# Starting the next token group's input projection beside the current group's top-k and routing

## The chip, the cores and the metric

One core of a Trainium2 chip runs the whole program. The metric is the device time of one execution in microseconds (us). TensorE (PE) does the matrix products, VectorE (DVE) elementwise work, reductions and top-8 searches, ScalarE (ACT) activations and copies, GpSimd (POOL) issues the gathers of expert rows, and SyncE (SP) issues nearly all other transfers. The matrices are float32.

## The reference, cut to what matters

One decoder layer is applied to 512 prompt tokens and 64 sample tokens. Each token's row of 2048 numbers passes through an input projection, two mixers (latent attention and gated linear attention), an output projection, the PEER expert layer and a gated embedding.

```
xn = rmsnorm(x, norm_mix);  z = xn @ w_in                      # 2048 x 3920, split for the two mixers
mix = concat(mla(z), gla(z)) @ w_out;  h = x + mix
xf = rmsnorm(h, norm_ffn)                                       # PEER:
q = (xf @ peer_w_q)                                             # 8 heads x 2 sides x 128
s1, s2 = q[:, :, 0] @ keys1.T, q[:, :, 1] @ keys2.T             # 128 scores for each head and side
v1, i1 = top_k(s1, 16);  v2, i2 = top_k(s2, 16)
top_s, sel = top_k(v1 + v2 (16 x 16 sums), 16)
e = i1[sel // 16] * 128 + i2[sel % 16];  gate = softmax(top_s)
h = h + sum over head, k of gate * gelu(xf . peer_u[e]) * peer_v[e]   # 128 gathered row pairs for each token
y = h + sigmoid(rmsnorm(h) @ w_ple_gate) * (p @ w_ple_proj)
```

## The kernel before, in words

**Tiles and groups.** The 576 tokens are five tiles: tiles 0 to 3 hold 128 prompt tokens each, tile 4 the 64 sample tokens. Three groups, [0], [1, 2] and [3, 4], pass one after the other through a front part: norm and `w_in` in two half passes, latent attention, linear attention, `w_out`, norm, queries, key scores, top-k and routes. A `w_in` pass streams 16 slabs of 128 rows through four slab buffers `W`, and TensorE multiplies every slab with the group's transposed rows (L682). All of the front part lives in one large buffer `front`, and its stages use the same places again: `H` and `Y` hold rows, `G` a gain, `zst` (the staging of z on its way to memory) is `H`, and the top-k tables `topv` and `topi` lie at `h0`, in `H` too.

**Gathered rows.** For every tile and head a unit of 16 `peer_u` and 16 `peer_v` gathers brings one expert row for each token (128 x 2048 numbers, 1.05 MB) into a ring of 8 buffers. VectorE takes each in one instruction: L1572, a dot product, for `peer_u`; L1597, scaled and added, for `peer_v`. There are 36 units (the sample tile is packed into 4), so 1152 gathered rows. GpSimd may gather for a head only when its expert indices are there, that is, after `route` of that tile and head.

**What sets the order.** Every engine executes its own list in order, and semaphores tie the lists together. VectorE's front work is a generator (`woven`) cut into steps at each `yield`. The table `ROWS_BEFORE` says for each step how many gathered rows are taken before it, and `STEPS_BEFORE` does the same for ScalarE in steps before each unit's gelu. So both tables fix by hand where, in the stream of gathered rows, a front step stands. If a step's input is late, VectorE stands still, gathered rows included.

**The boundary between groups.** After a group's key scores (L990) the scores stay in the eight PSUM banks. VectorE's `best_keys` (L1225 to L1242) finds the 16 best of 128 for each head and side there, both tiles of the group together; `route` (L1440 to L1491) combines them for two heads of the first tile at a time and, at the end, for all 8 heads of the second tile. TensorE starts the next group's first transposes only when `topk_done` counts all 16 searches of the group. SyncE loads the next group's x rows only when all of its routes are ready (`route_ready`, L453), ScalarE waits for that too, and the `w_in` slabs stand behind the x rows in SyncE's queue.

Of the kernel before, what the change touches and what calls it, by code (L numbers as in the profile page):

```python
# [21 lines left out]
ACT = mybir.ActivationFunctionType  # L22
# [5 lines left out]
P = 128  # L28
# [49 lines left out]
ROUTES = [r for g in GROUPS for t in g for r in ([(t, h, h + 2) for h in range(0, PH, 2)] if t == g[0] else [(t, 0, PH)])]  # L78
# [26 lines left out]
for _u in range(UNITS):  # L105
# [92 lines left out]
def build(nc, a, o, c):  # L198

    ctx = ExitStack()  # L200
    with ctx:
# [75 lines left out]
        selhf, sellf, e1, e2, gtop = [carve(P) for _ in range(5)]  # L277
        gsum = carve(PH)
        ixs_hi, gts_hi = carve(64)[0:NS].bitcast(U32), carve(64)[0:NS]
        assert used[0] <= y0  # L280
        cand, candw = Y, G
        oneh = candw

# [1771 lines left out]
```

## Time and profile before

| | |
|---|---|
| three timed runs | 4744.69, 4750.98, 4751.55 us; median 4750.98 |
| profiled execution, own time | 4747.69 us |
| its span in the trace | 4745.9 us |
| busy in the span | PE 2297.8, DVE 3408.7, ACT 506.9, POOL 2046.9 us |
| transfers | 1607.72 MB, mean 339 GB/s |

The page gives the whole span; its lines of digits cut it into 40 slices of about 119 us, with the busy share of each engine and of the 16 DMA engines in tenths. The other views give single instructions with their start, the chain of work, or the busy time of each engine within stretches that the reader chooses; a DMA share of 1.01 there means that all 16 DMA engines were busy throughout.

### The profile page before, as it was taken

What the parts mean: (1) busy time and instruction counts of PE and PEld (TensorE: products, weight loads), DVE (VectorE), ACT (ScalarE), POOL (GpSimd) and SP (SyncE); (2) the same over time, 40 slices, a digit from 0 to 9 for tenths busy, and PEclk for the clock granted to TensorE, in tenths of its full rate; (3) what the DMA queues carried; (4) which work ended last, traced back from release to release, by engine and by line L of the source; (5) the groups of instructions that cost most, each with busy time, mean ns of one, the idle gap of its engine ahead of it and who ended that gap; (6) DMA issues with size and microseconds to landing.
All of it is one profiled execution on the core that took longest, in us unless ns stands there. A gap on an engine that the chain in (4) does not pass through costs nothing.

```text
span 4745.9 us, 24855 instructions
## 1 busy us (share of the span) xinstructions
PE 2297.8 (48%) x7542; PEld 1261.5 (27%) x7542; DVE 3408.7 (72%) x3845; ACT 506.9 (11%) x962; POOL 2046.9 (43%) x1172
## 2 busy tenths in 40 slices
PE   8566296743875099261565642487309100000825
PEld 3335142423354033131232321235304000000311
DVE  0222955868667965797877799866896899988683
ACT  0110100212010000110221212001000000000100
POOL 0000423342442143575554474434123788888351
PEclk9678598656887599565677775688759655555967
DMA  8246699775997399999999998999739999999996
GB/s 300 103 183 221 276 420 418 277 274 187 412 420 296 134 420 421 365 378 339 372 355 363 338 393 300 361 406 419 286 143 421 414 422 422 421 402 422 421 406 217
DMA packets 262253, 1607.72 MB, mean 339 GB/s; under 512 B 35380, under 2 KB 53045, under 8 KB 92072
## 3 DMA queue, kind: packets, MB, share of 16 engines
q0 software_dynamic: 167936, 1222.71, 65.2%
q1 hardware_dynamic: 92872, 374.40, 21.0%
q10 hardware_dynamic: 1312, 9.03, 0.5%
q8 instruction: 59, 0.97, 0.1%
q14 instruction: 74, 0.61, 0.0%
HBM read 1562.91 MB, written 42.56 MB: 338 GB/s over the span
## 4 chain that ended last, share of the span: by engine, by line
PE 32%; DVE 28%; DMA 16%; POOL 15%; issue 5%; ACT 2%; SPq 1%; DVEq 0%; ACTq 0%; POOLq 0%
PE bank L682 21%; POOL ring L1997 15%; DVE ring L1572 8%; DVE total L1597 7%; DMA ring<-in_peer_u,idx_all 5%; PE bank L981 4%; DMA ring<-in_peer_v,idx_all 4%; DMA front<-in_peer_w_q 1%; PE bank L660 1%; DVE front L1059 1%; PE bank L793 1%; DMA front<-z_dram 1%; PE bank L792 1%; PE bank L810 1%; DVE front L1239 1%
## 5 line engine op out<-in xcount | busy, mean ns | idle before, releaser
L1597 DVE SCALAR_TENSOR_TENSOR total<-ring,gate_all,total 128x2048 f32<-128x2048 f32 x571 | 1342.1, 2350 | 318.5 <-DMA ring<-in_peer_v,idx_all 255.6
L1572 DVE CUSTOM_DVE_ANT_0 ring<-ring,xrow 128x2048 f32<-128x2048 f32 x576 | 1319.7, 2291 | 338.7 <-DMA ring<-in_peer_u,idx_all 278.1
L1997 POOL DMA_INDIRECT ring<-in_peer_u,idx_all x576 | 1004.3, 1744 | 1170.0 <-DVEq L1575 642.5
L1997 POOL DMA_INDIRECT ring<-in_peer_v,idx_all x576 | 1032.9, 1793 | 911.6 <-DVEq L1600 427.3
L682 PE MATMUL bank<-front 128*128 128x512 f32 (+3 forms) x2560 | 1104.9, 590 | 6.1 <-ACT front L1701 2.4
L660 PE MATMUL bank<-ident,front 128*128 128x128 f32 (+1 forms) x320 | 68.2, 402 | 1477.2 <-DVE front L1059 1160.5
L682 PEld LDWEIGHTS bank<-front 128*128 128x128 f32 (+1 forms) x2560 | 454.0, 181 | 651.3 <-issue 645.3
L660 PEld LDWEIGHTS bank<-ident,front 128*128 128x128 f32 (+1 forms) x320 | 55.1, 218 | 1492.9 <-DVE front L1059 1158.9
L981 PE MATMUL bank<-front 128*128 128x128 f32 (+2 forms) x1536 | 261.2, 333 | 18.5 <-DMA front<-in_peer_w_q 13.6
L981 PEld LDWEIGHTS bank<-front 128*128 128x128 f32 x1536 | 243.2, 194 | 36.5 <-DMA front<-in_peer_w_q 18.5
L1989 POOL DMA_DIRECT2D xrow<-xn_dram x6 | 3.6, 597 | 512.2 <-DVEq L1501 512.2
L1973 ACT ACTIVATE dots<-dots 128x16 f32<-128x16 f32 x36 | 7.8, 216 | 1339.4 <-DVE dots L1572 1338.6
L1095 DVE RECIPROCAL ms<-ms 128x1 f32<-128x1 f32 (+1 forms) x5 | 0.8, 162 | 182.3 <-ACT ms L1670 182.2
L860 PE MATMUL bank<-front 128*64 128x512 f32 x64 | 45.6, 803 | 105.1 <-DVE front L1263 95.6
L1055 DVE RECIPROCAL st<-st 128x1 f32<-128x1 f32 (+1 forms) x20 | 3.2, 162 | 123.6 <-ACT st L1661 122.3
L934 PE MATMUL bank<-front 128*128 128x128 f32 (+1 forms) x288 | 44.3, 327 | 81.8 <-DVE front L1326 69.2
L847 PE MATMUL bank<-ident,front 128*128 128x128 f32 x256 | 56.6, 323 | 51.2 <-DMA front<-in_cache_k_inv_rms 51.2
L879 PE MATMUL bank<-ident,front 64*128 64x64 f32 (+1 forms) x136 | 20.3, 317 | 120.3 <-ACT front L1886 109.5
L740 PE MATMUL bank<-front 128*128 128x384 f32 (+1 forms) x160 | 71.0, 610 | 12.7 <-DMA front<-in_w_uv 11.1
L885 PE MATMUL bank<-front 128*64 128x256 f32 x256 | 73.9, 460 | 2.4 <-ACT front L1897 2.4
L1225 DVE MAX8 front<-bank 128x8 f32<-128x128 f32 x80 | 20.7, 291 | 75.7 <-PE bank L990 70.2
L719 PE MATMUL bank<-ident,front 128*128 128x128 f32 (+1 forms) x20 | 5.1, 408 | 140.4 <-DVE front L1101 86.7
(283 smaller groups left out, 2520.7 us busy)
## 6 DMA issues: line engine op xcount, KB each, us to landing
front<-in_w_in SPq DMA_DIRECT2D x96, 980.0 KB
front<-in_w_out SPq DMA_DIRECT2D x48, 1024.0 KB
front<-in_peer_w_q SPq DMA_DIRECT2D x48, 1024.0 KB
front<-in_w_ple_gate SPq DMA_DIRECT2D x48, 1024.0 KB
front<-in_cache_kv_latent SPq DMA_DIRECT2D x128, 128.0 KB
front<-in_w_uq SPq DMA_DIRECT2D x6, 1536.0 KB, 10.2
ring<-in_peer_u,idx_all POOLq DMA_INDIRECT x576
ring<-in_peer_v,idx_all POOLq DMA_INDIRECT x576
```

The lines of the kernel that those rows point to most:

```text
L660: mm = e.transpose(bank[6 + m % 2][:, j * P:j * P + R], src, ident[:R, :R])
L682: mm = e.matmul(bank[4 * sl + c][:R, 0:ncol], XT[:, k, sl * P:sl * P + R], W[:, n % SLABS, c * ncol:(c + 1) * ncol], start=(k == 0), stop= ...
L740: mm = e.matmul(bank[j][:R, 0:2 * QK], cqT[:, slot(t), k, 0:R], wq[:, k, j * 2 * QK:(j + 1) * 2 * QK], start=(k == 0), stop=(k == 3))
L792: e.matmul(S[:, 0:nk], QTn[:, h, :], KTn[:, h, 0:nk], start=True, stop=False)
L793: e.matmul(S[:, 0:nk], QTr[r, h // 2, :], KTr[r, h // 2, 0:nk], start=False, stop=False)
L810: mm = e.matmul(bank[4][:, h * DV:(h + 1) * DV], pT[:, h % 2, kt * P:(kt + 1) * P], V[:, kt, h * DV:(h + 1) * DV], start=(kt == 0), stop=( ...
L847: e.transpose(bank[k][:, j * P:(j + 1) * P], latb[:, pg, k * P:(k + 1) * P], ident[:, :])
L885: e.matmul(bank[7][0:NS, 0:KVR], pTs[:, pg, :], latb[:, pg, :], start=(pg == 0), stop=False)
L981: mm = e.matmul(bank[j][:, 0:ntok], W[:, n % SLABS, at:at + P], XT[:, k, 0:ntok], start=(k == 0), stop=(k == KD - 1))
L1572: e.tensor_tensor_reduce(out=ring[:, b, :], in0=ring[:, b, :], in1=xrow[:, t % 2, :], scale=1.0, scalar=0.0, op0=ALU.mult, op1=ALU.add, ac ...
L1597: e.scalar_tensor_tensor(out=total, in0=ring[:, b, :], scalar=c1, in1=total, op0=ALU.mult, op1=ALU.add).then_inc(s("summed"), 1)
L1997: e.indirect_dma_start(out=ring[:, k % RING, :], out_offset=None, in_=a[("peer_u", "peer_v")[side]][0], in_offset=bass.IndirectOffsetOnAxi ...
```

## The change

- **Scores leave PSUM.** After the queries ScalarE copies the key scores of both tiles, bank by bank, into `SC`, which is `H` (new semaphore `scores_sb`; it waits until `H` has been stored). The top-k tables move behind `Y` and `G`.
- **The next group starts earlier.** x rows of groups 1 and 2 no longer go to `H` but to slab buffers 2 and 3 (`in_rows`). SyncE loads them once the query slabs are used up; slabs 2 and 3 of the next pass then wait for the norm. On VectorE the next group's norm stands between the first two heads' top-k and the first route (`first_route`), on ScalarE its squares stand before the first route (`rows_in`). z of the next group is evacuated by `z_rows`, in two parts within `other_routes`; since z is staged in `H`, the first part waits until all top-k of the current group are done. SyncE's load of z for the latents (L474 after) now carries the wait for all routes.
- **Top-k tile by tile**, one head (both sides) at a time, from SBUF; the key scores are computed tile by tile.
- **Routes of 2 and 6 heads** for a group's first tile instead of 2, 2, 2, 2. The first route has its own scratch (`cand_first`, 512 numbers twice); the others keep `Y` and `G` and so wait until the next group's rows have been transposed.
- **Both order tables are new.**

```diff
-ROUTES = [... ([(t, h, h + 2) for h in range(0, PH, 2)] if t == g[0] else [(t, 0, PH)])]
+ROUTES = [... ([(t, 0, 2), (t, 2, PH)] if t == g[0] else [(t, 0, PH)])]
...
+        def in_rows(t):
+            return H[:, slot(t), :] if t in GROUPS[0] else W[:, SLABS - MT + slot(t), :]
...
+                    if name[:4] == "in0_" and name != "in0_0" and SLABS - MT <= k < SLABS:
+                        e.wait_ge(s("normed"), NORMS["x", GROUPS[int(name[4:])][k - SLABS + MT]] + 1)
...
                 if g:
-                    e.wait_ge(s("route_ready"), sum(1 for t, _, _ in ROUTES if t < tiles[0]))
+                    e.wait_ge(s("slabs_used"), PASSES[f"in0_{g}"])
...
                 if g:
-                    e.wait_ge(s("topk_done"), 2 * PH * g)
+                    e.wait_ge(s("scores_sb"), 4 * tiles[0])
                 norm_transposes("x", tiles)
...
+            def first_route(g):
+                first = GROUPS[g][0]
+                yield from best_keys(first, 0, 2)
+                if g < LAST:
+                    yield from norm_rows("x", GROUPS[g + 1])
+                yield from route(first, 0, 2)
+
+            def other_routes(g):
+                first = GROUPS[g][0]
+                yield from best_keys(first, 2, PH)
+                yield from route(first, 2, PH)
+                for t in GROUPS[g][1:]:
+                    yield from best_keys(t, 0, PH)
+                    yield from route(t, 0, PH)
...
+            def z_rows(g, half):
+                e.wait_ge(s("slabs_used"), PASSES[f"in{half}_{g}"] + KD)
+                if half:
+                    e.wait_ge(s("z_stored0"), 16 * (tiles[-1] + 1))
+                elif g:
+                    e.wait_ge(s("topk_done"), PH * tiles[0])
...
+                e.wait_ge(s("h_stored"), 16 * (tiles[-1] + 1))
+                for sl, t in enumerate(tiles):
+                    for q in range(4):
+                        e.wait_ge(s("key_scores"), 4 * t + q + 1)
+                        e.copy(SC[:ROWS[t], sl, q * BANK:(q + 1) * BANK], bank[4 * sl + q][:ROWS[t], :]).then_inc(s("scores_sb"), 1)
```

**SyncE at the first boundary** (after the queries of tile 0). Before, the x rows of tiles 1 and 2 wait for the routes, and 32 slabs of `w_in` follow:

```order
L432 DMA front<-in_peer_w_q 128x2x1024 [waits slabs_used] x12
L453 DMA front<-in_x_prompt 128x2048 [waits route_ready]
L453 DMA front<-in_x_prompt 128x2048
L454 DMA front<-in_norm_mix 128x2048
L423 DMA front<-in_w_in 128x1960 [waits slabs_used] x32
```

Of the changed kernel, at the same place:

```order
L435 DMA front<-in_peer_w_q 128x2x1024 [waits slabs_used] x12
L456 DMA front<-in_x_prompt 128x2048 [waits slabs_used]
L456 DMA front<-in_x_prompt 128x2048
L457 DMA front<-in_norm_mix 128x2048
L426 DMA front<-in_w_in 128x1960 [waits slabs_used] x2
L426 DMA front<-in_w_in 128x1960 [waits normed,slabs_used] x2
L426 DMA front<-in_w_in 128x1960 [waits slabs_used] x28
```

The x rows now wait for TensorE's last query slab only, and two of the 32 slabs wait for the norm.

**TensorE at the first boundary.** Before, behind the last key scores:

```order
L990 MATMUL bank<-keysT,front 128x128 x3
L990 MATMUL bank<-keysT,front 128x128 [waits qT_evacuated]
L990 MATMUL bank<-keysT,front 128x128 x3
L990 MATMUL bank<-keysT,front 128x128 [waits qT_evacuated]
L990 MATMUL bank<-keysT,front 128x128 x3
L660 MATMUL bank<-ident,front 128x128 [waits nt_evacuated,normed,topk_done]
```

After:

```order
L995 MATMUL bank<-keysT,front 128x128 x3
L995 MATMUL bank<-keysT,front 128x128 [waits qT_evacuated]
L995 MATMUL bank<-keysT,front 128x128 x3
L995 MATMUL bank<-keysT,front 128x128 [waits qT_evacuated]
L995 MATMUL bank<-keysT,front 128x128 x3
L665 MATMUL bank<-ident,front 128x128 [waits nt_evacuated,normed,scores_sb]
```

The first transpose of the next group, with the whole `w_in` pass behind it, no longer waits for the top-k.

**VectorE at the second boundary** (groups 1 and 2). Before, the norm (L1055, L1059) stands after the last route of group 1 (L1491) and five gathered rows (L1572):

```order
L1491 TENSOR_TENSOR gate_all<-front 128x128
L1572 ISA ring,dots<-ring,xrow 128x2048 [waits dve_own,rows_landed7]
L1572 ISA dots 128x1
L1572 ISA ring,dots<-ring,xrow 128x2048 [waits dots_done,rows_landed0]
L1572 ISA dots 128x1
L1572 ISA ring,dots<-ring,xrow 128x2048 [waits dots_done,rows_landed1]
L1572 ISA dots 128x1
L1572 ISA ring,dots<-ring,xrow 128x2048 [waits dots_done,rows_landed2]
L1572 ISA dots 128x1
L1572 ISA ring,dots<-ring,xrow 128x2048 [waits dots_done,rows_landed3]
L1572 ISA dots 128x1
L1055 RECIPROCAL st<-st 128x1 [waits dots_done,rms_ready]
```

After, it stands between the top-k of the first two heads (up to L1236) and the first route (from L1438), with four gathered rows (L1604) around it:

```order
L1234 MAX_INDEX front<-front 128x8
L1236 CAST front<-front 128x32 [waits dve_own]
L1604 SCALAR_TENSOR_TENSOR total<-ring,gate_all,total 128x2048 [waits rows_landed1,topk_done]
L1604 SCALAR_TENSOR_TENSOR total<-ring,gate_all,total 128x2048 [waits summed,rows_landed2]
L1060 RECIPROCAL st<-st 128x1 [waits summed,rms_ready]
L1065 SCALAR_TENSOR_TENSOR front<-front,st 128x2048 [waits gain_loaded,dve_own]
L1604 SCALAR_TENSOR_TENSOR total<-ring,gate_all,total 128x2048 [waits rows_landed3]
L1604 SCALAR_TENSOR_TENSOR total<-ring,gate_all,total 128x2048 [waits summed,rows_landed4]
L1060 RECIPROCAL st<-st 64x1 [waits summed,rms_ready]
L1065 SCALAR_TENSOR_TENSOR front<-front,st 64x2048 [waits dve_own]
L1438 TENSOR_TENSOR front<-front 128x512
```

The top-k of the other six heads of tile 1, that of tile 2, and all routes of group 1 now stand behind the norm.

**Where front steps stand in the stream**: gathered rows (of 1152) ahead of each, counted in VectorE's order.

| step | before | after |
|---|---|---|
| first latent step of group 1 (L1095 before) | 80 | 46 |
| norm before `w_out`, group 1 | 161 | 155 |
| first top-k of group 1 | 235 | 225 |
| end of the last route of group 1 | 247 | 256 |
| first latent step of group 2 | 317 | 273 |
| norm before `w_out`, group 2 | 672 | 637 |
| first top-k of group 2 | 743 | 709 |
| first embedding norm | 767 | 791 |

## Rows read from the trace of the kernel before

**Rows 1.** Page of the whole program: span, busy times, 40 slices, chain

```profile
span 4745.9 us, 24855 instructions
...
PE 2297.8 (48%) x7542; PEld 1261.5 (27%) x7542; DVE 3408.7 (72%) x3845; ACT 506.9 (11%) x962; POOL 2046.9 (43%) x1172
...
DVE  0222955868667965797877799866896899988683
...
DMA  8246699775997399999999998999739999999996
```

**Rows 2.** Windows (from:to, length, busy us of each engine, clock, DMA share, GB/s)

```profile
434.00:564.00 130.00, 7.74 (x50) 6.81 (x49) 111.79 (x317) 12.64 (x23) 36.99 (x25) 0.53 0.55 215
564.00:677.00 113.00, 111.58 (x273) 52.16 (x273) 72.92 (x49) 4.04 (x9) 43.55 (x33) 0.96 1.01 420
...
786.00:1204.00 418.00, 185.96 (x594) 118.21 (x594) 312.98 (x379) 88.89 (x181) 147.25 (x86) 0.60 0.72 269
...
1483.00:1640.00 157.00, 5.34 (x48) 5.15 (x47) 149.25 (x508) 2.13 (x6) 17.45 (x16) 0.53 0.32 120
...
1899.00:3108.00 1209.00, 537.00 (x2019) 305.78 (x2019) 997.25 (x907) 210.92 (x380) 676.66 (x361) 0.65 0.97 357
```

**Rows 3.** Same columns, dot-product rows (L1572) alone: x counts two records each

```profile
1784.00:1899.00 115.00, 29.91 (x26) 1.00 1.01 421
3700.00:4300.00 600.00, 257.68 (x224) 0.50 1.01 416
```

**Rows 4.** Same columns, weighted-sum rows (L1597) alone

```profile
1784.00:1899.00 115.00, 35.28 (x15) 1.00 1.01 421
3700.00:4300.00 600.00, 292.86 (x125) 0.50 1.01 416
```

**Rows 5.** Timeline at the first boundary (start us, us, engine, line)

```profile
434.98 0.30 DVE L1225 MAX8 front<-bank 128x8 f32<-128x128 f32 x1 [63.99 <-PE bank L990]
...
463.05 2.29 DVE L1572 CUSTOM_DVE_ANT_0 ring<-ring,xrow 128x2048 f32<-128x2048 f32 x1 [9.25 <-DMA ring<-in_peer_u,idx_all]
...
538.54 0.82 SPq L453 DMA_DIRECT2D front<-in_x_prompt  x2
...
545.95 1.91 ACT L1660 ACTIVATE front<-front 128x2048 f32<-128x2048 f32 x1 [13.01 <-DMA front<-in_x_prompt]
```

**Rows 6.** Chain in order of time: the w_in passes (start us, us)

```profile
567.96 107.54 PE bank L682 x256
...
1670.57 112.77 PE bank L682 x256
```

**Rows 7.** Timeline of VectorE at the second boundary

```profile
1483.02 0.50 DVE L1225 MAX8 front<-bank 128x8 f32<-128x128 f32 x2 [3.07 <-PE bank L990]
...
1495.50 0.69 DVE L1440 TENSOR_TENSOR front<-front 128x512 f32<-128x512 f32 x1
...
1506.42 0.18 DVE L1491 TENSOR_TENSOR gate_all<-front 128x32 f32<-128x32 f32 x1
...
1606.20 2.29 DVE L1440 TENSOR_TENSOR front<-front 128x2048 f32<-128x2048 f32 x1
...
1640.05 0.28 DVE L1491 TENSOR_TENSOR gate_all<-front 128x128 f32<-128x128 f32 x1
```

**Rows 8.** Timeline of VectorE: first latent steps of groups 1 and 2, third boundary

```profile
835.23 0.16 DVE L1095 RECIPROCAL ms<-ms 128x1 f32<-128x1 f32 x1 [16.30 <-ACT ms L1670]
...
1918.84 0.17 DVE L1095 RECIPROCAL ms<-ms 128x1 f32<-128x1 f32 x1 [25.16 <-ACT ms L1670]
...
3384.76 0.49 DVE L1225 MAX8 front<-bank 128x8 f32<-128x128 f32 x2
```

**Rows 9.** Groups by form (count | busy us, mean ns | idle before)

```profile
L1225 DVE MAX8 front<-bank 128x8 f32<-128x128 f32 x64 | 17.6, 295 | 75.7 <-PE bank L990 70.2
L1235 DVE MAX8 front<-front 128x8 f32<-128x128 f32 x64 | 17.2, 290 | 1.7
...
L1831 ACT COPY front<-bank 128x512 f32<-128x512 f32 x16 | 8.1, 611 | 83.8 <-PE bank L682 83.8
```

More of the change, by code:

```diff
@@ L460, in mixer_loads @@
                     e.wait_ge(s(f"z_stored{half}"), 16 * (tiles[-1] + 1))
+                if g:
+                    e.wait_ge(s("route_ready"), sum(1 for t, _, _ in ROUTES if t < tiles[0]))
                 if g == 0:
@@ L1085, in mixer @@
                 tiles = GROUPS[g]
-                nt = len(tiles)
-                yield
-                yield from norm_rows("x", tiles)
                 yield
@@ L1226, in best_keys @@
                     link(ins)
                     yield
-                    for sl in range(nt):
-                        R = ROWS[tiles[sl]]
-                        e.max_index(topu[:R, sl, 0:8], top(sl)[:, 0:8], sco(sl))
-                        ins = e.match_replace(out=swork[:R, sl, :], in_to_replace=top(sl)[:, 0:8], in_values=sco(sl), imm_value=LOWEST)
+                    for i in range(2):
+                        e.max_index(topu[:R, i, 0:8], top(i)[:, 0:8], sco(i))
+                        ins = e.match_replace(out=swork[:R, i, :], in_to_replace=top(i)[:, 0:8], in_values=sco(i), imm_value=LOWEST)
@@ L1232, in best_keys @@
                     link(ins)
                     yield
-                    for sl in range(nt):
-                        ins = e.max(top(sl)[:, 8:16], swork[:ROWS[tiles[sl]], sl, :])
+                    for i in range(2):
+                        ins = e.max(top(i)[:, 8:16], swork[:R, i, :])
                     link(ins)
-                    for sl in range(nt):
-                        R = ROWS[tiles[sl]]
-                        ins = e.max_index(topu[:R, sl, 8:16], top(sl)[:, 8:16], swork[:R, sl, :])
+                    for i in range(2):
+                        ins = e.max_index(topu[:R, i, 8:16], top(i)[:, 8:16], swork[:R, i, :])
@@ L1248, in best_keys @@
                     yield
-                    if n % 4 == 3:
-                        yield
             def sample():
@@ L1438, in route @@
                 ti = topi[:R, sl, 2 * lo:2 * hi, :].rearrange("p (h w) k -> p h w k", w=2)
+                if lo == 0 and hi < PH:
+                    cand, candw = cand_first, candw_first
+                else:
+                    cand, candw = Y, G
+                    if t < GROUPS[LAST][0]:
+                        nxt = next(tiles for tiles in GROUPS if tiles[0] > t)
+                        yield
+                        e.wait_ge(s("nt_transposed"), 4 * (NORMS["x", nxt[-1]] + 1))
+                oneh = candw
                 cv = cand[:R, 0:nk * TOPK].rearrange("p (h i j) -> p h i j", h=nh, i=TOPK)
@@ L1543, in _ @@
             routed = {}
+            for x in norm_rows("x", GROUPS[0]):
+                pass
             for x in mixer(0):
                 pass
-            for x in route(0, 0, 2):
+            for x in first_route(0):
                 pass
@@ L1679, in pT_copy, with rows_in @@
                 e.copy(pT[:, h % 2, 0:(t + 1) * P], bank[2 + h % 2][:, 0:(t + 1) * P]).then_inc(s("pT_sb"), 1)
+            def rows_in(g):
+                tiles = GROUPS[g]
+                yield from norm_squares("x", tiles, lambda t: e.wait_ge(s("rows_loaded"), 16 * (3 * tiles[0] + len(tiles))))
+                yield
+            def z_rows(g, half):
+                tiles = GROUPS[g]
+                yield
+                e.wait_ge(s("slabs_used"), PASSES[f"in{half}_{g}"] + KD)
[3 more added lines that the diff above has]
+                    e.wait_ge(s("topk_done"), PH * tiles[0])
+                else:
+                    e.wait_ge(s("normed"), NORMS["x", tiles[-1]] + 1)
+                for sl, t in enumerate(tiles):
+                    R = ROWS[t]
+                    for c in range(4):
+                        e.copy(zst[:R, sl, c * IN_BANK:(c + 1) * IN_BANK], bank[4 * sl + c][:R, 0:IN_BANK]).then_inc(s("z_read"), 1)
+                    e.wait_ge(s("z_read"), 8 * BEFORE[g] + 4 * (len(tiles) * half + sl + 1))
+                    e.dma_start(z_dram[rows(t), half * IN_HALF:(half + 1) * IN_HALF], zst[:R, sl, 0:IN_HALF])\
+                        .then_inc(s(f"z_stored{half}"), 16)
+                yield
             def mixer(g):
@@ L1840, in mixer @@
                     yield
+                e.wait_ge(s("h_stored"), 16 * (tiles[-1] + 1))
+                for sl, t in enumerate(tiles):
+                    for q in range(4):
+                        e.wait_ge(s("key_scores"), 4 * t + q + 1)
+                        e.copy(SC[:ROWS[t], sl, q * BANK:(q + 1) * BANK], bank[4 * sl + q][:ROWS[t], :]).then_inc(s("scores_sb"), 1)
+                    yield
             def sample():
@@ L1952, in _ @@
             e.copy(keysT[:, :, :], four(bank[0])[:, 0:2]).then_inc(s("keysT_sb"), 1)
+            for x in rows_in(0):
+                pass
+            for half in range(2):
+                for x in z_rows(0, half):
+                    pass
             for x in mixer(0):
                 pass
-            for x in route(0, 0, 2):
+            for x in first_route(0):
                 pass
```

121 lines of the change are left out of this document (45 added, 76 removed), and 74 rows, old and new, of the table ROWS_BEFORE.

## The prediction

> **What bounds the kernel now.** I read the page first. The span is 4745.9 us; VectorE is busy for 3408.7 of it and idle for 1337; the DMA line stands at 9 in 26 of 40 slices, the VectorE line at 8 or 9 in 18 of 40, and they are seldom low together [rows 1]. No engine is the bound throughout: the program alternates between stretches that lack transfers and stretches that lack VectorE. So I cut the span into windows at the boundaries and passes [rows 2]. While group 1's top-k and routes run (1483 to 1640) VectorE is busy 149 of 157 us and the DMA share is 0.32. In the `w_in` half pass from 564 it is the reverse: TensorE busy 112 of 113 us, DMA share 1.01, VectorE 73 of 113, waiting for gathered rows. These two kinds of stretch stand behind each other at both boundaries, and the change lays them beside each other.
>
> The second thing to read is the price of a gathered row. Where rows alone run, 125 weighted sums and 224/2 = 112 dot products take 600 us, 2.53 us a row; in a `w_in` half pass 15 + 13 rows take 115 us, 4.1 us a row [rows 3, 4]. The total is fixed at 1152 rows, so a front part that ends earlier has fewer rows behind it: the saving in its chain is partly paid back in rows, at 2.53 us each.
>
> Third, the chain across a boundary. At the first one the first search starts at 435.0, the first gathered row at 463.1, x rows are issued only at 538.5 and read at 546.0 (7.4 us later), and `w_in` starts at 568.0 [rows 5, 6]. At the second one the searches start at 1483.0, the last route ends at 1640.3, and `w_in` starts at 1670.6 [rows 6, 7]. The first latent steps come at 835.2 and 1918.8, the third boundary at 3384.8 [rows 8].
>
> **Step 1, the first boundary.** The query slabs are used up just before the first search (435.0). From there x rows take 7.4 us (443), four score copies 0.61 us each [rows 5, 9] are done by then, and the norm of two tiles goes as it did before, 568.0 - 546.0 = 22 us from the first square to the first product; part of those 22 was a wait behind gathered rows, so I take 18. `w_in` then starts at 461 instead of 568: **-107**. Slabs 2 and 3 are issued only after the norm, but slabs 0 and 1 hold 2 x 107.5/16 = 13 us of TensorE work. The price is that the first route, and with it the first gathered row, comes 13 us later (two norms between); it is paid once in VectorE idle time and is covered since this stretch's rows are not the last to finish: 240 rows must be taken before tile 1 begins, and there is room for them (step 2). The two half passes stay 107.5 us each, as TensorE bounds them. The z staging waits for all top-k (by about 520) and half 0 ends at 568; z for the latents waits for the route of heads 2 to 7, which stands by row 35, near 620, and half 1 ends at 677. Both are hidden; the cover is 45 and 55 us. The first latent step moves from 835 to about 728.
>
> **Step 2, group 1's mixers.** The order puts 155 - 46 = 109 rows between the first latent step and the norm before `w_out`, where 161 - 80 = 81 stood. 28 more rows are 28 x 2.5 = 70 us of VectorE. The window from 786 to 1204 has 418 - 313 = 105 us of VectorE idle and a DMA share of 0.72 [rows 2], so there is room, but a front step that finds a row under way waits for it. Bounds: 0 (all in idle time) and 70 (none). I take 15, nearer the lower end, as the idle time is one and a half times what is asked. From there to the key scores both orders hold about as many rows (70 and 74) beside passes that TensorE bounds. The second boundary comes at 1483 - 107 + 15 = **1391**.
>
> **Step 3, the second boundary.** Score copies end 9 us behind the first key score, then square, norm, transposes and the same again for tile 2: I take 31 us (the 22 above and the 9), so `w_in` starts at 1422 instead of 1670.6: **-249**. The half passes take 112.8 us each [rows 6] and end at 1648. Over the same time VectorE has, from 1391: 16 heads' searches at 3.12 us for two searches (1483.0 to 1495.5 holds four double ones), 50 us; a route of two heads 11.1 us and of eight 34.1 us [rows 7]; a line through these two, 3.4 + 3.84 for each head, gives 26.5 for six, so 72 us of routes; norms and waits 10; and rows 225 to 256, 78 us. Sum 210, so the last route ends near 1600, 48 us before z can be read; and all top-k are done near 1391 + 140 = 1531, when half 0 ends at 1535. That cover is only 4 us; without it TensorE stands between the halves for as long as the top-k is late. The order leaves 17 rows from there to the latent step, at 4.1 us 70 us, to 1670: it fits. The first latent step of group 2 comes at 1918.8 - 249 = **1670**.
>
> The two transfers that stand beside each other now: a group's `w_in` is 32 slabs of 0.98 MB, 31 MB, 75 us at 420 GB/s; the DMA engines were idle for 0.68 x 157 = 107 us in the stretch of top-k [rows 2]. So there is room for it.
>
> **Step 4, group 2 up to the third boundary.** Before, 743 - 317 = 426 rows in 1466 us; after, 709 - 273 = 436. The DMA share is 0.97 there [rows 2], so ten more rows cost up to 25 us; I take 25 (bounds 0 and 25). The third boundary comes at 3384.8 - 249 + 25 = **3161**.
>
> **Step 5, the rest.** 1152 - 709 = 443 rows stand behind it instead of 409: 34 x 2.53 = **+86**. Routes of 2 + 6 heads instead of 4 x 2 save 3 x 11.1 - 26.5 = 6.8 us of VectorE for each group; I count it here once (**-7**), since at the other two boundaries VectorE's time is already compared with the passes.
>
> **Reading scores from SBUF.** MAX8 on a bank takes 295 ns and on SBUF 290 [rows 9]: 5 ns for each of 240 searches and replacements, 1 us, nothing. The 20 score copies are 12 us of ScalarE, which is busy for 507 of 4746 us [rows 1].
>
> The Trainium skill (VectorE: DVE Perf Modes, section on the TRN2 errata) gives a Vector operation a fixed 120 cycles from PSUM and 58 from SBUF. By it the 240 operations would become 65 ns shorter each, an estimated 15 us; this case's rows show 5 ns, and the sum goes by them. By the page alone it would come to 4590.
>
> **Sum.** Against the profiled execution: 4747.7 - 249 + 25 + 86 - 7 = 4602.7. That execution is 3.3 us under the median of the runs shown, so I predict **4605** us, 3.1% less. In one line: time = 4748 + (shift of group 2's first latent step) + 104. The change pays only if that step comes more than 104 us earlier.
>
> **The rivals.**
>
> *The mixers stretch (A).* VectorE runs in order, and both mixer stretches now hold more rows. If the 28 rows cost their full 70 us (step 2's upper bound) and the thin cover in step 3 fails by 20 us, the time is 4605 + 55 + 20 = 4680. For it: ScalarE's late answers already hold VectorE (16.3 and 25.2 us before the latent steps [rows 8]). Against: 105 us of idle time in that window.
>
> *The transfers collide less than I think (B).* If the added rows of steps 2 and 4 fall wholly into idle time, 4605 - 15 - 25 = 4565.
>
> *Slower (C).* The new order places front steps 34 to 44 rows earlier. If `w_in` does not start earlier, VectorE meets a latent step whose z has not come and stands there, with rows waiting in the ring. The mechanism would be the x rows in slab buffers 2 and 3: SyncE holds the whole `w_in` queue until the norm, which stands in VectorE's list behind a search and in ScalarE's behind the score copies. Should that give no shift at all, the time is 4748 + 104 = 4852; from a shift under 104 us on the change loses. Against it: nothing in the new chain of norm waits for a gathered row at the first boundary, and for four at the second.
>
> *It does nothing (D).* If the DMA engines were the bound everywhere, moving 31 MB would give back what it takes. The share of 0.32 speaks against it.
>
> **How the numbers follow.** The forecast (4550 to 4640) gets 0.63, A (4640 to 4735) 0.19, B or better (under 4550) 0.05, C 0.10, D 0.03. A measurement of this kernel tells about 0.2%, 9.5 us, from no change. So faster 0.87, same 0.03, slower 0.10. The range for 8 in 10 runs from B's end to A's: 4550 to 4685.
>
> **What would show it.** Right: `w_in` of group 1 starts near 461 and of group 2 near 1422; the windows there show DMA shares well above 0.55 and 0.32 with VectorE above 0.9; TensorE has no gap between half passes; latent steps near 728 and 1670; third boundary near 3161; VectorE idle for about 1337 - 145 + 20 = 1210 us in all. Wrong: a gap between the half passes that ends with the top-k (step 3's cover); waits for ScalarE or TensorE in the mixers that grow by more than the rows' idle time shrinks (step 2); a first latent step of group 2 after 1815 (C).

## The result and the profile after

The changed kernel takes 4596.15 us in the median of 4 runs (4589.09 to 4601.08); the kernel before, run beside it on the same chip, 4750.88 us (4744.69 to 4751.55). The ratio is 0.9676, with a 95% interval of [0.9659, 0.9693]: 155 us or 3.2% less. Forecast were 4605 us and 3.1%. The profiled execution took 4598.28 us.

The page of the kernel after, its rows that answer to [rows 1]:

```profile
span 4596.3 us, 24756 instructions
...
PE 2297.8 (50%) x7542; PEld 1261.9 (27%) x7542; DVE 3388.4 (74%) x3713; ACT 506.0 (11%) x968; POOL 2194.5 (48%) x1172
...
DVE  0231858888568879968778898568996899998683
...
DMA  8347998877998899999999989998669999999996
```

TensorE's busy time is the same to 0.1 us and VectorE's 20 us less, so hardly any work went; what went is waiting. VectorE is idle for 4596.3 - 3388.4 = 1208 us (1337 before). In the DMA line the two 6s in slices 4 and 5 have become 7 and 9, and the 3 in slice 14 an 8; these were the two stretches of top-k.

Windows of the kernel after, columns as in [rows 2]: the wait for the first norm, the two `w_in` half passes, the mixers, and the two passes up to the second boundary; then the same at the second boundary, and the two long stretches that end the kernel.

```profile
434.00:462.00 28.00, 12.15 (x72) 10.32 (x71) 15.29 (x55) 13.13 (x27) 0.00 (x0) 0.70 0.68 257
462.00:568.00 106.00, 105.43 (x256) 48.23 (x256) 89.70 (x219) 4.96 (x8) 50.47 (x30) 1.00 0.94 386
568.00:674.00 106.00, 105.52 (x256) 48.35 (x256) 65.36 (x47) 3.69 (x9) 39.66 (x26) 1.00 1.01 420
693.00:1114.00 421.00, 185.23 (x594) 118.83 (x594) 369.86 (x413) 87.26 (x174) 213.86 (x108) 0.60 0.80 301
1114.00:1386.00 272.00, 245.16 (x873) 163.15 (x874) 171.24 (x120) 26.56 (x55) 97.35 (x72) 0.95 1.01 420
1386.00:1418.00 32.00, 10.85 (x75) 9.55 (x74) 22.76 (x52) 13.50 (x23) 7.88 (x5) 0.66 1.01 390
1418.00:1532.00 114.00, 113.44 (x256) 39.93 (x255) 107.59 (x346) 1.99 (x5) 26.77 (x14) 0.98 0.73 278
1532.00:1643.00 111.00, 110.80 (x256) 39.15 (x256) 98.63 (x125) 3.71 (x9) 55.75 (x29) 1.00 0.95 387
1667.00:3138.00 1471.00, 761.35 (x2851) 441.59 (x2852) 1181.71 (x1034) 220.15 (x409) 805.33 (x440) 0.70 0.98 370
3138.00:4597.00 1459.00, 338.84 (x861) 150.31 (x859) 1195.12 (x1175) 56.96 (x97) 891.99 (x444) 0.61 0.91 369
```

In [rows 2] the search stretch 1483 to 1640 had VectorE busy for 149 of 157 us with TensorE at 5 us and a DMA share of 0.32. Here, from 1418 to 1532, VectorE is busy for 108 of 114 us and TensorE for 113 of the same 114, and the DMA share is 0.73. One sign that the prediction named did not come at the first boundary: VectorE was to be busy above 0.9 there, and from 462 to 568 it is busy for 89.7 of 106 us, 0.85.

Timeline rows of the kernel after, first and second boundary and third, in order of time (L1098 is the latent step, L1060 at 1114.0 the norm before `w_out`, L1222 a boundary's first search):

```profile
434.78 0.82 SPq L456 DMA_DIRECT2D front<-in_x_prompt  x2
...
436.97 0.49 DVE L1222 MAX8 front<-front 128x8 f32<-128x128 f32 x2 [64.83 <-ACT front L1859]
...
443.20 1.91 ACT L1668 ACTIVATE front<-front 128x2048 f32<-128x2048 f32 x1 [3.63 <-DMA front<-in_x_prompt]
...
452.53 1.91 ACT L1668 ACTIVATE front<-front 128x2048 f32<-128x2048 f32 x1
...
461.89 105.55 PE L687 MATMUL bank<-front 128*128 128x490 f32 x256 [0.68 <-ACT front L1675]
...
478.83 2.29 DVE L1579 CUSTOM_DVE_ANT_0 ring<-ring,xrow 128x2048 f32<-128x2048 f32 x1 [10.38 <-DMA ring<-in_peer_u,idx_all]
...
693.29 0.16 DVE L1098 RECIPROCAL ms<-ms 128x1 f32<-128x1 f32 x1 [28.76 <-ACT ms L1678]
...
702.97 0.16 DVE L1098 RECIPROCAL ms<-ms 128x1 f32<-128x1 f32 x1 [1.72 <-ACT ms L1678]
...
1114.02 0.16 DVE L1060 RECIPROCAL st<-st 128x1 f32<-128x1 f32 x1
...
1385.59 0.49 DVE L1222 MAX8 front<-front 128x8 f32<-128x128 f32 x2 [1.60 <-ACT front L1859]
...
1417.70 113.74 PE L687 MATMUL bank<-front 128*128 128x490 f32 x256 [0.46 <-ACT front L1675]
...
1532.18 110.80 PE L687 MATMUL bank<-front 128*128 128x490 f32 x256 [0.75 <-ACT front L1709]
...
1667.20 0.16 DVE L1098 RECIPROCAL ms<-ms 128x1 f32<-128x1 f32 x1 [17.86 <-ACT ms L1678]
...
3138.24 0.49 DVE L1222 MAX8 front<-front 128x8 f32<-128x128 f32 x2 [3.41 <-ACT front L1859]
```

`w_in` starts at 461.9 and 1417.7 instead of 568.0 and 1670.6 [rows 6], 106 and 253 us earlier, and between its half passes TensorE waits 0.75 us. Group 2's first latent step comes at 1667.2 instead of 1918.8 [rows 8]: 251.6 us earlier, of which 155 arrive at the end.

Reading the kernel before beside this showed two rows of [rows 8] that I had taken for something else. Its timeline of VectorE has these as well; the middle one is the norm before `w_out` of group 1, which ends the mixers:

```profile
808.49 0.16 DVE L1095 RECIPROCAL ms<-ms 128x1 f32<-128x1 f32 x1 [13.40 <-ACT ms L1670]
...
1201.75 0.16 DVE L1055 RECIPROCAL st<-st 128x1 f32<-128x1 f32 x1 [1.25 <-ACT st L1661]
...
3368.22 0.49 DVE L1225 MAX8 front<-bank 128x8 f32<-128x128 f32 x2 [3.09 <-PE bank L990]
```

So 835.2 is the latent step of group 1's second tile, and the first one stands at 808.5. And the third boundary's first search is at 3368.2; 3384.8 is the fourth of that group.

### The profile page after: what moved, and what is told of

It is laid out like the page before. It is cut to its first block, busy times and chain, and to the rows that moved or that the text cites. A ratio compares the mean times of both kernels' runs of the same rounds, so it can differ in the third digit from the quotient of the medians.

```text
span 4596.3 us, 24756 instructions
## 1 busy us (share of the span) xinstructions
PE 2297.8 (50%) x7542; PEld 1261.9 (27%) x7542; DVE 3388.4 (74%) x3713; ACT 506.0 (11%) x968; POOL 2194.5 (48%) x1172
## 4 chain that ended last, share of the span: by engine, by line
PE 35%; DVE 28%; POOL 14%; DMA 13%; issue 6%; ACT 3%; SPq 1%; DVEq 0%; ACTq 0%; POOLq 0%
PE bank L687 24%; POOL ring L2029 14%; DVE total L1604 9%; DVE ring L1579 9%; PE bank L986 5%; DMA ring<-in_peer_v,idx_all 3%; DMA ring<-in_peer_u,idx_all 3%; DMA front<-in_peer_w_q 1%; PE bank L665 1%; DVE front L1065 1%; PE bank L709 1%; ACT front L1668 1%; PE bank L798 1%; DMA front<-z_dram 1%; DVE front L1364 1%
## 5 line engine op out<-in xcount | busy, mean ns | idle before, releaser
L2029 POOL DMA_INDIRECT ring<-in_peer_v,idx_all x576 | 1094.3, 1900 | 934.4 <-DVEq L1607 441.3
L2029 POOL DMA_INDIRECT ring<-in_peer_u,idx_all x576 | 1090.6, 1893 | 893.1 <-DVEq L1582 388.1
L1604 DVE SCALAR_TENSOR_TENSOR total<-ring,gate_all,total 128x2048 f32<-128x2048 f32 x571 | 1341.9, 2350 | 228.9 <-DMA ring<-in_peer_v,idx_all 173.7
L1098 DVE RECIPROCAL ms<-ms 128x1 f32<-128x1 f32 (+1 forms) x5 | 0.8, 161 | 175.1 <-ACT ms L1678 175.0
L1060 DVE RECIPROCAL st<-st 128x1 f32<-128x1 f32 (+1 forms) x20 | 3.2, 162 | 166.7 <-ACT st L1669 166.4
L815 PE MATMUL bank<-front 128*128 128x128 f32 x160 | 45.0, 445 | 60.0 <-ACT front L1687 60.0
L1222 DVE MAX8 front<-front 128x8 f32<-128x128 f32 (+1 forms) x80 | 19.4, 284 | 73.7 <-ACT front L1859 69.8
```

The costliest lines, as they stand in the source:

```text
L1604: e.scalar_tensor_tensor(out=total, in0=ring[:, b, :], scalar=c1, in1=total, op0=ALU.mult, op1=ALU.add).then_inc(s("summed"), 1)
L2029: e.indirect_dma_start(out=ring[:, k % RING, :], out_offset=None, in_=a[("peer_u", "peer_v")[side]][0], in_offset=bass.IndirectOffsetOnAxi ...
```

## The experiments

Two theories stood at the start. **T**, the prediction's: the time is group 2's first latent step plus a constant as long as the order tables stay the same. For the changed kernel's tables it is about 2930 us, 102 more than before (rows that the shortened front leaves behind). Each us by which `w_in` starts earlier and the latent step follows is a us of time. **R**, the rival: much of what the top-k and `w_in` gain by standing side by side comes from idle time that would be used anyway, so taking the overlap away costs about half.

**Holding `w_in` back, one boundary at a time.** TensorE waits, between the norm's transposes and the first product of `w_in`, until all top-k of the current group are done. All else stays, the order tables too.

```diff
                 norm_transposes("x", tiles)
+                if g == 1:
+                    e.wait_ge(s("topk_done"), PH * tiles[0])
                 project(f"in0_{g}", "x", tiles, IN_BANK)
```

> The changed kernel, with one wait added on TensorE: after the transposes of group 1's rows, the first w_in product waits until every top-k of group 0 is done. In the changed kernel that is at 520 us of the trace and w_in starts at 462, so w_in, the first latent step of group 1 (693) and the second boundary (1386) should each come 58 us later. Theory T (time follows the shift of the front chain one for one, the order tables being fixed): 4596 + 58 = 4654 us, ratio to before 0.980. Rival R (the idle time of VectorE and of the DMA engines decides, and what is lost at one boundary is caught up while the gathered rows run): at most half of it, 4625 us or less.

With `g == 2` in its place:

> The same wait, only ahead of group 2's w_in: it waits until every top-k of group 1 is done. That is at 1521 us in the changed kernel, where w_in starts at 1418, so w_in and the first latent step of group 2 (1667) should come 104 us later. Theory T: 4596 + 104 = 4700 us, ratio to before 0.989. Rival R: the rows gathered while w_in waits go at full speed and give back half: 4645 us or less.

With `if g:`, at both:

> Both waits at once. My line in the prediction was: time = 4748 + (shift of group 2's first latent step against the kernel before) + 104. Here that shift should be -252 + 58 + 104 = -90, so T expects 4758 us, within 0.3% of the kernel before: the start at the top-k's end is where the change breaks even. Rival R: the two losses overlap in the rows' idle time, 4700 us or less.

Measured: hold_g1 4654.65 us (4647.27 to 4659.62), ratio 0.9802 [0.9787, 0.9817]; hold_g2 4689.54 us (4687.34 to 4698.38), ratio 0.9882 [0.9867, 0.9897]; hold_both 4744.59 us (4740.5 to 4754.51), ratio 0.9994 [0.9985, 1.0003]. Timeline of TensorE and VectorE with hold_g1:

```profile
519.21 106.97 PE L687 MATMUL bank<-front 128*128 128x490 f32 x256 [58.10 <-DVE front L1238]
...
747.50 0.16 DVE L1100 RECIPROCAL ms<-ms 128x1 f32<-128x1 f32 x1 [81.69 <-ACT ms L1680]
```

and with hold_g2:

```profile
1521.96 113.20 PE L687 MATMUL bank<-front 128*128 128x490 f32 x256 [103.88 <-DVE front L1238]
...
1761.72 0.16 DVE L1100 RECIPROCAL ms<-ms 128x1 f32<-128x1 f32 x1 [71.47 <-ACT ms L1680]
```

and with hold_both, at the second boundary:

```profile
1577.15 113.13 PE L687 MATMUL bank<-front 128*128 128x490 f32 x256 [103.88 <-DVE front L1238]
...
1816.63 0.16 DVE L1100 RECIPROCAL ms<-ms 128x1 f32<-128x1 f32 x1 [71.24 <-ACT ms L1680]
```

`w_in` is 57.3 and 104.3 us later than in the changed kernel, the latent step behind it 54.2 and 94.5, and the end of the profiled span 54.6 and 89.1. In between VectorE stands 81.7 and 71.5 us at the latent step, where it stood 28.8 and 17.9: it has run through the rows that the order gives it and can take no more. R is refuted for these order tables. They were made for an early `w_in`; no run gives the held kernels a table of their own, so how much of the loss another order would win back is not shown. hold_both keeps every other part of the change (score copies, tile by tile, 2 + 6 heads, new order, x rows early) and gives the old time back to within 0.2%: its group 2 latent step is at 1816.6, 102.2 us before the old one. That is the break-even of 104 us that the prediction named.

The latent steps move less than `w_in` (54.2 of 57.3 us, 94.5 of 104.3), and hold_both ends 13 us under its expected 4758. The missing part lies behind the second half pass: z is stored, loaded again and squared before the latent step. These are the times from the end of that half pass to the step, with the DMA share in them:

| kernel, group | us | DMA share |
|---|---|---|
| before, 1 and 2 | 26.7, 23.9 | 1.01, 1.01 |
| after, 1 and 2 | 19.6, 24.2 | 0.83, 1.01 |
| routes_2222 (below), 1 | 25.9 | 1.01 |
| hold_g1, 1; hold_g2, 2 | 15.1, 15.0 | 0.71, 0.69 |
| hold_both, 1 and 2 | 14.9, 14.8 | 0.71, 0.69 |

While VectorE stands, GpSimd gathers nothing (its last gather in hold_g2 is issued at 1690.6), the transfers thin out, and z comes back sooner. That the gathers in flight hold up z is read from this table; no run changes them alone.

**Four routes of two heads again** (ROUTES as before, the loop cut in four; the second, third and fourth route follow each other, without rows between the second and the third; the first entry of `STEPS_BEFORE` is 1 instead of 0).

```diff
-ROUTES = [... ([(t, 0, 2), (t, 2, PH)] if t == g[0] else [(t, 0, PH)])]
+ROUTES = [... ([(t, h, h + 2) for h in range(0, PH, 2)] if t == g[0] else [(t, 0, PH)])]
...
-                yield from route(first, 2, PH)
+                for h in (2, 4):
+                    for x in route(first, h, h + 2):
+                        pass
+                yield from route(first, 6, PH)
+                yield
...
```

> The changed kernel with the first tile of each group routed 2 heads at a time four times again (2, 2, 2, 2) in place of 2 and 6; searches, boundaries and the order tables as in the changed kernel, and the three routes stand where the one of six heads stood. Each group gives VectorE 6.8 us more. If only the third boundary's VectorE time is on the path (as the prediction counted), 4596 + 7 = 4603; if the second boundary's is too, 4610; if all three, 4617 us.

Measured: 4609.5 us (4604.19 to 4616.3), ratio 0.9708 [0.9695, 0.9721]: 13 us more than the changed kernel (15 by the ratios). VectorE is busy for 3406.7 us, 18.3 more, 6.1 for each group. Its last route of group 0 ends at 640.2 instead of 631.2. The cover of 55 us that step 1 gave this route was 43 in the changed kernel, against half 1's end (673.7), and is 34 here, so nothing waits for the route itself. Yet the first latent step of group 1 moves by 6.7 us: the gathers behind the route come later too, the last one is issued at 674.3 instead of 665.7, and the step follows half 1's end by 25.9 us instead of 19.6 (table above). The mixers and the passes behind them add 3.5 us, the second boundary nothing (from `w_in` to the latent step 249.6 us, 249.5 in the changed kernel), and the stretch behind group 2's latent step 3.7. Each of these two is less than the two profiled spans of the changed kernel differ by (4596.3 and 4601.8).

**The first route between the two norms.** In the changed kernel VectorE does both norms of the next group and then the route; here one norm, the route, the other norm, on ScalarE too.

```diff
                 if g < LAST:
-                    yield from norm_rows("x", GROUPS[g + 1])
+                    yield from norm_rows("x", GROUPS[g + 1], GROUPS[g + 1][:1])
                 yield from route(first, 0, 2)
+                if g < LAST:
+                    yield from norm_rows("x", GROUPS[g + 1], GROUPS[g + 1][1:])
```

> The changed kernel with one route moved: at the first two boundaries VectorE and ScalarE do the norm of the next group's first tile, then the route of two heads, then the norm of the second tile; in the changed kernel both norms come first. VectorE waits 6.7 us between the two norms at the first boundary and the route takes 11 us, so I expect w_in(1) at about 466 (461.89 in the changed kernel) and the first gathered row at about 468 instead of 478.83. Theory T (the end follows the shift of group 2's first latent step, about 102 us added): w_in starts 4 us later at each boundary, the routes end where they did or up to 9 us earlier, so between 4590 and 4605 us in the median, a latent step of group 2 between 1661 and 1676. A rival, that the gather stream's start and not w_in carries the boundary: the 10 us come through at both boundaries, about 4580 us.

Measured: 4601.06 us (4596.16 to 4606.97), ratio 0.969 [0.9676, 0.9703]. `w_in` starts 4.6 and 12.5 us later, group 2's latent step 7.1 us later, the span ends 4.0 us later. The first gathered row is 8.5 us earlier, and that buys nothing. In the medians it and the changed kernel can't be told apart, as the intervals overlap:

```profile
466.44 104.06 PE L687 MATMUL bank<-front 128*128 128x490 f32 x247 [0.68 <-ACT front L1677]
...
470.29 2.29 DVE L1581 CUSTOM_DVE_ANT_0 ring<-ring,xrow 128x2048 f32<-128x2048 f32 x1 [8.34 <-DMA ring<-in_peer_u,idx_all]
...
1674.32 0.16 DVE L1098 RECIPROCAL ms<-ms 128x1 f32<-128x1 f32 x1 [25.96 <-ACT ms L1680]
```

**Fewer rows in the mixers.** Only the order table differs: 14 rows that stood between group 1's first latent step and its mixture's norm stand behind that norm.

```diff
 ROWS_BEFORE = [
...
-    142, 142, 144, 144, 144, 144, 145, 145, 145, 145, 145, 145, 146, 155, 155, 155, 156, 156, 156, 187, 187, 191, 191,
-    225, 225, 225, 225, 225, 225, 225, 225, 225, 227, 227, 227, 229, 229, 229, 229, 229, 229, 229, 229, 229, 229, 229,
...
+    116, 116, 116, 116, 116, 116, 117, 117, 117, 117, 117, 117, 117, 117, 117, 117, 117, 117, 117, 129, 129, 129,
...
+    130, 130, 130, 130, 130, 130, 130, 131, 131, 131, 131, 132, 132, 132, 132, 132, 132, 133, 141, 141, 141, 142,
+    142, 142, 173, 173, 177, 177, 225, 225, 225, 225, 225, 225, 225, 225, 225, 227, 227, 227, 229, 229, 229, 229,
```

> The changed kernel with nothing changed but the order table: 14 of the 109 gathered rows that stand inside group 1's mixers are moved behind them, into group 1's w_out and query passes (its mixture's norm comes after 141 rows instead of 155; the first top-k step after 225 as before). Theory 1, a row's price depends on the stretch: inside the mixers a row costs about 0.9 us (31 more rows stretched them by 27 us), in the passes the DMA engines are at 0.95 to 1.0, so a row costs the 2.5 us that it takes on them: the mixers 13 us shorter, the passes 35 us longer, the second boundary at about 1405 instead of 1383 and the time about 4618 us. Theory 2, the passes are bound by TensorE (VectorE is busy 85 of 143 us and 76 of 113 us in them) and the rows fit in their idle time: second boundary at about 1370, time about 4583 us. In between, if rows cost the same in both: 4596.

Measured: 4645.8 us (4640.52 to 4655.17), ratio 0.9787 [0.9773, 0.98], 50 us more than the changed kernel. Its windows for the mixers and for the two passes:

```profile
693.00:1125.00 432.00, 188.74 (x594) 120.29 (x594) 338.51 (x388) 87.17 (x174) 185.00 (x94) 0.59 0.69 259
1125.00:1443.00 318.00, 247.29 (x859) 164.57 (x860) 203.19 (x144) 25.78 (x54) 118.91 (x85) 0.88 1.01 418
```

The passes grew from 272 to 318 us at the same 418 to 420 GB/s: 318 x 418 - 272 x 420 makes 18.7 MB more. The 14 rows are 14.7 MB of it, 35 us at this rate or 2.5 us a row; the rest are the x rows and the first two `w_in` slabs of group 2, 4 MB that now arrive ahead of the second boundary instead of behind it, and `w_in` follows 25.8 us behind the first search and not 32.1. That is theory 1's price, and the window below shows how TensorE stopped being the bound: in the last 48 us ahead of the boundary it is busy for 3.9 us, where it was 47.5.

```profile
1395.00:1443.00 48.00, 3.88 (x19) 3.34 (x18) 32.40 (x28) 2.57 (x10) 24.59 (x15) 0.55 1.01 403
```

ScalarE's gelu, ahead of the copies of the queries in its list, waits there for the unit's last dot product, and the key scores wait for these copies. But the mixers did not shrink by 13 us, they grew by 11, and the reason is my table. It made a clump of 12 rows where the old one has single rows and then eight. In the timeline of VectorE eleven dot products and a weighted sum, without a front step between them, stand ahead of the copies that ScalarE waits for (one and three in the changed kernel); the last of them:

```profile
1022.47 2.35 DVE L1606 SCALAR_TENSOR_TENSOR total<-ring,gate_all,total 128x2048 f32<-128x2048 f32 x1
...
1030.32 0.68 DVE L1404 COPY front<-bank 128x512 f32<-128x512 f32 x1
...
1054.74 0.69 DVE L1285 TENSOR_SCALAR front<-bank 128x512 f32<-128x512 f32 x1 [16.35 <-ACT front L1811]
```

ScalarE waits 39.5 us there (16.4 in the changed kernel), and VectorE pays with 16.4 us at the next step that needs ScalarE. So the run shows the price of a row in passes that transfers bound; it doesn't show what one costs in the mixers, since count and places were changed at once. Theory 1's 4618 was 28 us too low: the passes took 12 us more than its 35, the mixers 24 more than its -13, and 6 came back ahead of `w_in`. The end again follows the latent step: 51.4 us later, the span 47.5.

**A shorter way into `w_in`.** In route_between an earlier first row bought nothing, so what is left to shorten is the way into `w_in`. The timeline of the changed kernel shows what holds it: the second tile's squares (452.5) wait until the first tile's norm, in the one buffer `Y`, has been transposed. Here ScalarE takes both squares in a row, the second's into `XT`, and VectorE writes the second norm in place, over the tile's x rows in the slab; TensorE transposes it from there, and the slab's next load waits for these transposes.

```diff
-                    e.scalar_tensor_tensor(out=Y[:R, 0:width], in0=src, scalar=inv, in1=G[:R, 0:width],
+                    dst = src if in_place(use, t) else Y[:R, 0:width]
+                    e.scalar_tensor_tensor(out=dst, in0=src, scalar=inv, in1=G[:R, 0:width],
...
+                        link(e.activation(XT[:R2, 0:KD // 2, :], in_rows(tiles[1])[:R2, :].rearrange("p (k n) -> p k n", n=GT),
+                                          ACT.Square, accum_out=st[:R2, n2:n2 + 1]))
```

> The changed kernel with a shorter way into the w_in passes of groups 1 and 2: ScalarE takes the squares of both x tiles one after the other (the second one's squares go to the space of the transposed rows instead of the one norm buffer), and VectorE writes the second tile's norm over its own rows in the slab instead of waiting for the norm buffer to be transposed. In the changed kernel the second tile's squares start at 452.53, behind the copies of the first tile's transposes, and w_in(1) at 461.89. Worked out from its rows: first norm 445.8 to 448.2, its 3.7 us of transposes to 452, the second tile's 3.7 us right behind, w_in(1) at about 456, that is 6 us earlier at both boundaries. Theory T (the end follows the shift of group 2's first latent step one for one) gives 6 to 12 us less than the changed kernel run beside it, 4584 to 4590 us; 6 and not 12 if half of each shift is lost before the next latent step, as with route_between (w_in(1) 4.6 us later there, group 1's first latent step 2.1 us later). Rival, that the gather stream alone sets the boundary: no difference, within 2 us.

> The changed kernel once more, unaltered, as the measure for norm_in_place on the same chip: 4596 us, within 5 us.

Measured: norm_in_place 4588.01 us (4585.96 to 4596.24), ratio 0.9662 [0.9648, 0.9675]; the changed kernel beside it 4596.18 us (4593.44 to 4609.4), ratio 0.968 [0.9667, 0.9693]. Timeline of norm_in_place:

```profile
440.72 1.91 ACT L1684 ACTIVATE front<-front 128x2048 f32<-128x2048 f32 x1 [3.86 <-DMA front<-in_x_prompt]
...
442.96 1.89 ACT L1689 ACTIVATE front<-front 128x2048 f32<-128x2048 f32 x1
...
445.80 6.89 PE L672 MATMUL bank<-ident,front 128*128 128x128 f32 x32 [9.56 <-issue]
...
453.37 105.55 PE L694 MATMUL bank<-front 128*128 128x490 f32 x256 [0.67 <-ACT front L1675]
...
1659.05 0.16 DVE L1106 RECIPROCAL ms<-ms 128x1 f32<-128x1 f32 x1 [18.97 <-ACT ms L1700]
```

All 32 transposes run in one piece of 6.9 us. From the first square to `w_in` it takes 12.65 us instead of 18.69, the 6 us that were worked out. Group 2's latent step is 10.6 us before that of the run beside it (1669.67) and the span 15.2 us shorter; in the medians it is 8 us. The two intervals overlap by a little (0.9667 to 0.9675), so the gain of 0.2% is likely, not certain. It is the fastest version here.

**One line through all of them.** Group 2's first latent step, the profiled span, and the difference:

| kernel | latent step | span | difference |
|---|---|---|---|
| before | 1918.8 | 4745.9 | 2827.1 |
| norm_in_place | 1659.1 | 4586.6 | 2927.5 |
| after | 1667.2 | 4596.3 | 2929.1 |
| changed_again | 1669.7 | 4601.8 | 2932.1 |
| route_between | 1674.3 | 4600.3 | 2926.0 |
| routes_2222 | 1677.5 | 4610.3 | 2932.8 |
| rows_to_passes | 1718.6 | 4643.8 | 2925.2 |
| hold_g1 | 1725.2 | 4650.9 | 2925.7 |
| hold_g2 | 1761.7 | 4685.4 | 2923.7 |
| hold_both | 1816.6 | 4740.6 | 2924.0 |

The step moves over 157 us, the difference over 9.

## Why the prediction was right, step by step

Right in the mechanism, and 9 us off (4605 to 4596). Of these 9, 4.4 are the terms: against the profiled execution the sum was 4602.7, and 4598.3 came. The rest is no mechanism: the step from the profiled execution to the median added 2.3 us in the forecast, and in the measurement it takes off 2.1. The measured times stand in brackets.

- **Step 1.** `w_in` at 461 (461.9), group 0's top-k done by 520 (519.9), last route near 620 (631), half 1 ends at 677 (673.7; the second half pass took 105.5 us before too, and not 107.5), first gathered row 13 us later (15.8). The first latent step was to move from 835 to 728, and here a row was misread, as shown above: like with like, the second tile's moved from 835.2 to 703.0, and the first tile's from 808.5 to 693.3, 115 us and not 107. The extra 8 us are 2 us of a faster first half pass and 7 of z's way through memory, 26.7 us before and 19.6 after (table above), less the 1 us that `w_in` fell short of 107. The shorter distance between the two tiles, 9.7 us instead of 26.7, comes from SyncE. Before, its three loads behind the first z (L609 to L611) take 2.14, 12.77 and 4.31 us to issue, from 799.6 to 818.9, and the second tile's z load stands behind them; after, the same three (L614 to L616) take 0.60, 1.16 and 2.15 us.
- **Step 2.** The mixers were to stretch by 15 us, bounds 0 and 70. From the first latent step to the mixture's norm it was 393.3 us before and is 420.7 now: +27.4, for 28 more rows (81 before, 109 now, as forecast; the 31 in an expectation above came from a window that began too late). The term was sized too low, within its bounds: 1.0 us a row. That is the lower end of the price, as the two tiles also moved 17 us closer: counted from the second tile's step, the row that the prediction had read, the mixers grew by 44.4 us for 29 rows, 1.5 us a row. VectorE's idle time in the stretch fell from 88 to 51 us, so it held 37 of the 70 us and not 55. The passes behind, put at no change for "about as many" rows, took 271.6 us instead of 281.3: 4 rows fewer, 9.7 us less. So three terms were off, by -8 (the misread row), +12 (the mixers) and -10 us (the passes); they nearly cancel, by luck, and the second boundary came at 1385.6 (1391).
- **Step 3.** `w_in` at 1422 (1417.7), all top-k done at 1531 (1521), half 0 ends at 1535 (1531.4), last route 1600 (1604), latent step at 1670 (1667.2). The cover that I put at 4 us was 10, and TensorE's wait between the halves is 0.75 us. The gain hangs on this step and the first together: with `w_in` held to the end of the top-k at both boundaries nothing is left of it (hold_both). A slab of `w_in` is 128 x 1960 x 4 bytes, 1.00 MB, so the 32 are 32 MB and not 31, which changes nothing in the sum.
- **Step 4.** From the latent step to the third boundary: +25 predicted. With the right row for the third boundary it was 3368.2 - 1918.8 = 1449.4 us and is 3138.2 - 1667.2 = 1471.0: +21.6. The absolute 3161 was 17 too late for the misread row alone.
- **Step 5.** +86 for rows and -7 for the routes, +79: from the third boundary to the span's end it was 1377.7 us and is 1458.1, +80.4. The misread row stood in neither term, as it drops out of the sum; it spoiled two milestones and not the time. The routes were counted once, 7 us; routes_2222 puts them at 13 us in all. 6.7 of these arise at the first boundary, where the prediction called them hidden, and none at the second.
- **Reading scores from SBUF.** Its searches (L1222) take 285 ns each by form where those on a bank took 295 [rows 9], so 10 ns for 5. The second searches, on SBUF in both kernels, went from 290 to 285 ns as well, so no more than the forecast 5 ns belongs to the bank. The 65 ns that the cycles of the Trainium skill (VectorE: DVE Perf Modes, section on the TRN2 errata) would give are not there; the row was the better guide. No run here took the score copies away alone.
- **The rivals.** A's two halves: the mixers took 27 of 70 us, and the cover held. B needed a mixers term of 0. C's wait, the slabs behind the norm, never bound: between the norm of the second tile and the first product lie 7 us of transposes and copies, and TensorE then runs 105.55 us without a stop. The break-even from which C decides was right, as hold_both shows. D is refuted by the time itself; the mean rate rose from 339 to 350 GB/s.

What remains open: what a row in the mixers costs by its place, how much of the 27 us there is a matter of the order table, and what the new tables are worth apart from the early `w_in`.

## What to carry to other kernels

Where two kinds of stretch, one short of transfers and one short of vector work, stand behind each other, compare busy shares by window and lay them side by side; then find the one event through which everything later passes, and price the change by its shift minus what is paid back behind it. Work that an order table spreads over the program has a price by stretch: about 2.5 us a row where the DMA engines are full, 1.0 to 1.5 us in a stretch where they are at 0.7 to 0.8, and a clump ahead of a result that another engine waits for costs more than the rows. Before a milestone is built on a row, check that it is the first of its kind.

## What the runs showed of the hardware

- The same load took SyncE 12.77 us to issue in the kernel before (L610) and 1.16 us in the one after (L615). Around the first the DMA share was 1.02 (799 to 819); around the second it was 0.77 (686 to 694). GpSimd issued no gather during either, but the last one before was 6 us back in the first case (issued at 795.4) and 24 us in the second (665.7). In routes_2222 this load took 2.63 us (share 0.99). Group 2's, which brings more tiles, took 2.44 us before and 5.84 after, both at 1.01, and 0.65 in hold_g2 at 0.69. That a full set of DMA engines holds up the issue is the likely reason; it wasn't tried by itself.
- Storing z and reading it back, from the end of the second half pass to the latent step, took 14.8 to 15.1 us at a DMA share of about 0.7, 19.6 at 0.83 and 23.9 to 26.7 at 1.01 (table above).
- TensorE ran the first `w_in` half pass in 105.55 us with searches, routes and gathers beside it, and in 107.54 us before without the searches [rows 6]. The 2 us are the clock's: before, the first 7 us of the pass had a mean granted clock of 0.72, between the levels of 1.2 and 2.4 GHz, behind 28 us in which TensorE was busy for 7.5; after, it was 1.00 from the first product, behind 28 us with 12. The second half passes took 105.5 us in both kernels. At the second boundary the first half pass took 113.74 us with the searches and 112.77 without, with a clock of 0.58 and 0.72 in its first 7 us; norm_in_place and hold_g2 lie between, 112.88 us at 0.70 and 113.21 at 0.66. Both differences are what the clock gives, 7 x 0.28 = 2 us and 7 x 0.14 = 1 us, so laying the two side by side cost TensorE nothing else.
